# HGRN2 queries as two pairs of seven half-size products, between the transforms of the long convolutions

## The reference, cut to what matters

```python
proj = h @ p["w_in"]
(hg_q, hg_f_fwd, hg_f_bwd, hg_v, hg_g, ...) = _split(proj[..., D_CONV:], PLAIN_SPLITS)
uf = jnp.fft.rfft(uf32, n=2 * L, axis=1)
y = jnp.fft.irfft(uf * hf[None], n=2 * L, axis=1)[:, :L]
z = x1 * _fft_bidir_conv(v, filt[:, 0, 0], filt[:, 1, 0], p["hy_bias"][0])
y_a = x2 * _fft_bidir_conv(z, filt[:, 0, 1], filt[:, 1, 1], p["hy_bias"][1])
o_hg, s_hg = _scan_both_directions(
    _hgrn2_chunked, (heads(jax.nn.silu(hg_q), HG_DK), heads(hg_v, HG_DV)), ...)
```

## Time and profile before

| | us |
|---|---|
| median of 3 runs | 1392.11 (1391.52 to 1392.51) |
| profiled execution, first to last instruction | 1392.6 |
| TensorE busy in it | 1355.8 (97%) |
| VectorE busy | 600.6 |
| ScalarE busy | 390.8 |
| GpSimd busy | 313.7 |

### The profile page before, as it was taken

How to read it: one execution, slowest core, us unless ns; L and a number is a source line. 1 busy time by engine, 2 the same in 40 slices (tenths; PEclk the granted TensorE clock), 3 DMA queues, 4 the chain that set the end, 5 groups by cost and what they waited for, 6 DMA issues and landing times.

```text
span 1392.6 us, 20702 instructions
## 1 busy us (share of the span) xinstructions
PE 1355.8 (97%) x7716; PEld 950.3 (68%) x7716; DVE 600.6 (43%) x1347; ACT 390.8 (28%) x769; POOL 313.7 (23%) x248
## 2 busy tenths in 40 slices
PE   7999999999999999999999999999999999999996
PEld 2695898989988996788988875444445444444453
DVE  3467451885545486533322266333222332322224
ACT  3232221322544255233431141222112211221122
POOL 0431232243135553553333001101000000000001
PEclk9999999999999999999999999999999999999998
DMA  9640423133213336812144536999999999999992
GB/s 355 212 136 1 137 91 121 35 118 92 92 61 92 106 122 270 285 51 48 61 136 137 165 121 264 392 414 421 419 420 421 421 421 420 421 419 420 420 417 85
DMA packets 109744, 321.54 MB, mean 231 GB/s; under 512 B 12489, under 2 KB 72649, under 8 KB 81136
## 3 DMA queue, kind: packets, MB, share of 16 engines
q1 hardware_dynamic: 98416, 307.64, 57.6%
q0 software_dynamic: 2560, 8.81, 1.6%
q10 hardware_dynamic: 8704, 4.20, 1.1%
HBM read 320.08 MB, written 4.33 MB: 233 GB/s over the span
## 4 chain that ended last, share of the span: by engine, by line
PE 86%; DMA 9%; DVE 2%; ACT 1%; POOL 1%; issue 1%; SPq 0%; DVEq 0%; POOLq 0%
PE banks L650 21%; PE banks L617 20%; PE banks L2933 12%; DMA w<-in_exp_w 7%; PE banks L2980 7%; PE banks L2835 6%; PE banks L1057 3%; PE banks L2820 2%; PE banks L624 2%; PE banks L1201 1%; DMA ring<-in_ada_w 1%; PE banks L2828 1%; PE banks L769 1%; PE banks L889 1%; PE banks L701 1%; PE banks L1260 1%
## 5 line engine op out<-in xcount | busy, mean ns | idle before, releaser
L2933 PE MATMUL banks<-w,xg 128*64 128x512 f32 (+1 forms) x1312 | 235.8, 594 | 2.0 <-DMA w<-in_exp_w 1.9
L2933 PEld LDWEIGHTS banks<-w,xg 128*64 128x64 f32 (+1 forms) x1312 | 72.1, 126 | 150.9 <-issue 126.4
L650 PE MATMUL banks<-hT,ring 128*128 128x192 f32 x792 | 137.7, 327 | 0.2 <-DMA ring<-in_w_in 0.2
L3310 POOL DMA_INDIRECT fetched<-token_rows,row_of_place x32 | 32.1, 1004 | 443.2 <-DVE row_of_place L3111 433.1
L650 PEld LDWEIGHTS banks<-hT,ring 128*128 128x128 f32 x792 | 129.6, 190 | 2.1 <-DMA ring<-in_w_in 0.8
L2980 PE MATMUL banks<-w,hidT 128*64 128x512 f32 (+1 forms) x656 | 122.6, 600 | 0.3 <-DMA w<-in_exp_w 0.2
L2835 PE MATMUL banks<-y,selT 128*128 128x512 f32 x384 | 115.0, 415 | 0.0
L650 PE MATMUL banks<-x,ring 128*128 128x192 f32 x528 | 97.0, 327 | 0.9 <-ACT late L1377 0.9
L650 PE MATMUL banks<-x,combos 128*128 128x192 f32 x528 | 96.6, 326 | 0.0
L3122 DVE SCALAR_TENSOR_TENSOR hid<-banks,gslot,sil 128x256 f32<-128x256 f32 x33 | 16.0, 484 | 178.3 <-ACT sil L3015 177.7
L2835 PEld LDWEIGHTS banks<-y,selT 128*128 128x128 f32 x384 | 66.3, 189 | 35.1 <-issue 26.2
(11 more groups left out here) (482 smaller groups left out, 2033.4 us busy)
## 6 DMA issues: line engine op xcount, KB each, us to landing
w<-in_exp_w SPq DMA_DIRECT2D x198, 1024.0 KB, 13.9
ring<-in_w_in SPq DMA_DIRECT2D x46, 1024.0 KB, 5.5
ring<-in_ada_w SPq DMA_DIRECT2D x24, 1024.0 KB, 6.9
ring<-in_w_branch SPq DMA_DIRECT2D x8, 1024.0 KB, 6.6
ring<-in_w_out SPq DMA_DIRECT2D x4, 1024.0 KB, 6.6
arena<-in_sh_w SPq DMA_DIRECT2D x3, 1024.0 KB, 8.4
x<-in_x_sample SPq DMA_DIRECT2D x4, 512.0 KB, 8.3
token_rows<-whole_rows SPq DMA_DIRECT2D x3, 384.0 KB, 20.1
```

The costliest lines, as they stand in the source:

```text
L650: last = mm(out, lhsT=w[:, k, :], rhs=tokens[:, k, :], start=start and k == 0, stop=k == KD // 2 - 1, skip_group_check=not start)
L2933: ins = mm(ps[lo:hi, :], lhsT=xg[:, k, a_ * P + lo:a_ * P + hi], rhs=w13[:, a_, u, :, k, :], start=k == 0, stop=k == KD - 1)
L3310: nc.gpsimd.indirect_dma_start(fetched[:, a_, :], None, rows[:, :], bass.IndirectOffsetOnAxis(ap=row_of_place[:, 2 * a_:2 * a_ + 1], axis= ...
```

## The change

The queries join `PAIRS` between `hy_x2` and the forget gates. In each order TensorE runs `pair("hg_q", order)` in place of the two blocks of `project_T`. ScalarE keeps the partial results in `hq` itself; VectorE adds them up after that order's spectra, behind its wait for `s_spec`; and one silu over the whole of `hq` (128x1536), in place, follows the second `add_up`. VectorE waits for it (`s_queries`) before it adds up the first forget gates. The list of GpSimd's loop is `PAIRS`, so it prepares the queries' weights too.

```diff
@@ -419,7 +419,7 @@
-        PAIRS = [(name, h) for name in PAIRED[0:2] + FORGET for h in range(2)] + \
+        PAIRS = [(name, h) for name in PAIRED[0:2] + ("hg_q",) + FORGET for h in range(2)] + \
@@ -429,6 +429,8 @@
+            if name[0] == "hg_q":
+                return hq[:, 2 * name[1]:2 * name[1] + 2, :]
@@ -455,6 +457,7 @@
+        s_queries = sig("hgrn_queries_ready")
@@ -856,7 +859,7 @@
                 merge(0, order)
-                project_T("hg_q", "act", 2 * order, 2 * order + 2)
+                pair("hg_q", order)
                 pe.wait_ge(s_fconst.sem, 16 * N_FCONST)
                 pe.wait_ge(s_spec.sem, (order + 1) * NT)
@@ -1350,6 +1353,8 @@
             def block_sums_free(name):
 
+                if name[0] == "hg_q":
+                    return
@@ -1466,8 +1471,10 @@
                 merge_gate(0, j)
-                for c in (2 * j, 2 * j + 1):
-                    copy(hq[:, c, :], ("hg_q", c), ACT.Silu, src=banks.at(act, ("hg_q", c))[:, 0:T])
+                keep("hg_q", j)
+                keep_last("hg_q", j)
+            banks.emptied(act, ("hg_q", 1, "y"))
+            s_queries.on(on(flat(hq), flat(hq), ACT.Silu))
@@ -1981,6 +1988,7 @@
                 dve.wait_ge(s_spec.sem, s_spec.n)
+                add_up("hg_q", order)
                 if order == 0:
@@ -1993,7 +2001,7 @@
-            banks.emptied(dve, ("hg_q", CW - 1))
+            dve.wait_ge(s_queries.sem, 1)
             for name in FORGET:
```

## The result

| | before | changed |
|---|---|---|
| first comparison, median | 1392.31 us (6 runs, 1391.52 to 1395.13) | 1400.72 us (6 runs, 1396.89 to 1401.4) |
| ratio, 95% interval | | 1.0052 [1.0041, 1.0063] |
| second comparison, median | 1392.84 us (21 runs) | 1399.13 us (5 runs, 1398.32 to 1401.39) |
| ratio, 95% interval | | 1.0044 [1.0030, 1.0057] |
| profiled execution, span | 1392.6 us | 1399.6 us (first), 1399.0 us (second) |

The change made the kernel slower, as forecast, and by more: by the medians +8.4 us in the first comparison and +6.3 in the second, where the forecast was +5.25 and the range ended at +7.5. The ratios are taken over all runs and not from the two medians; that of the first comparison, 1.0052, is +7.2 us. So the median of 1400.72 lies 1.1 us above the range, and the time by the ratio just inside its upper end.

A forecast was written before the change was run, and what follows sets the result against it. TensorE was taken to bound the kernel, VectorE close behind. 2.44 us given back against new waits of 3.1 and 3.0 gave +3.65; one clock fall, 1.6, made +5.25 on 1392.11: 1397.4 us, range 1393.5 to 1399.6.

The forecast's parts named there:

- What bounds the kernel: Over the two convolutions, TensorE sets the time, with no wait ahead of either transform back; VectorE is close behind.
- the slack of VectorE: Ahead of the transforms back, VectorE's chain ends 1.50 us (order 0) and 2.56 us (order 1) before TensorE asks.
- The pair's own gain: Queries' products as a pair take 9.10 us, not 10.32: TensorE gains 1.22 us an order, 2.44 us in all.
- Four operations of GpSimd an order: Preparing weights for pairs puts four GpSimd operations among VectorE's eight long ones, costing 4.28 us an order.
- The price of a meeting: Each GpSimd operation beside a long VectorE one, both reading SBUF, costs VectorE 1.07 us; bounds nothing and 1.27.
- the old meeting at 108.08: In order 0, the forget gates' combinations no longer delay VectorE's L1962, which takes 0.95 us off its chain.
- What was costed at nothing: VectorE's adding up (about 1.2 us each time), ScalarE's copies and the silu (at most 1.7 us) delay nothing.
- Rival 1: VectorE's chain in both orders runs undisturbed by GpSimd; the whole 2.44 us stays, 1389.7 us; chance 9%.
- rival 2: Only two of four GpSimd operations an order meet VectorE's, 1391.5 us; with three, 1393.6; chance 13%, half for three.
- The clock: After one of TensorE's two new waits, its clock falls to half speed in the dense transforms, costing 1.6 us.
- the old fall: Clock drop at 391.80 in the profile before: 18 records took 3.83 us, not 2.34, so 1.5 us lost.
- two falls: The clock drops after both new waits ahead of the transforms back, costing 3.2 us: 1399.0 us; chance 18%.

The follow-up runs named there:

- foreign additions: Kernel before the change, with four unrelated GpSimd additions of 128x512 in SBUF added per order beside VectorE's long operations: 1398.76 us, ratio 1.0052.
- the two versions where nothing waits behind it: Changed kernel with GpSimd's three later operations held until the order's spectra, 1390.79 us; changed kernel with queries' pairs moved behind both convolutions, 1391.99 us.
- filler: Changed kernel with seven unused TensorE products ahead of each wait for the spectra: 1396.56 us, ratio 1.0026.
- held-back one: Changed kernel with GpSimd waiting for each order's spectra before preparing the next pair's weights: 1390.79 us, ratio 0.9986; again 1391.10 us, ratio 0.9993.

## Why the prediction was right, and where it was short

- **What bounds the kernel, and the slack of VectorE** (1.50 and 2.56 us): right. The four foreign additions met just this slack.
- **The pair's own gain**, 2.44 us: right; -2.43 and -2.44 in the two versions where nothing waits behind it.
- **Four operations of GpSimd an order, all among VectorE's long ones**: right, in place and number.
- **The price of a meeting**, 1.07 us: right for the first of an order, 2.29 - 1.22, but 0.95 for the three that follow (2.17 - 1.22). An order costs VectorE 3.9 us and not 4.28. The other row that I had, 0.95 for L1962, was as near, and a mean of the two would have been better. The waits, counted from start to start as in the forecast, were 2.80 and 2.69 us in place of 3.1 and 3.0 (2.63 and 2.52 as the profile counts idle time); the two shifts, without the late start, 1.57 and 1.54, together 3.11 in place of 3.65. By the rule of the Trainium skill ("SBUF — State Buffer", section "Who interferes with whom") taken literally, 1.27 each, the sum would have been further off.
- **That the old meeting at 108.08 goes**: right. No GpSimd operation stands there any more (idle for 16.46 us ahead of L2488), and the sum with it comes out.
- **What was costed at nothing**: right. The wait ahead of the second spectra is 0.78 us, where it was 0.79: `add_up` is covered. The silu has 1.48 us and ends 2.6 us after the second transform has begun, as its row in the timeline of ScalarE shows:

```profile
156.15 1.48 ACT L1477 ACTIVATE yT<-yT 128x1536 f32<-128x1536 f32 x1 [4.58 <-DVE yT L1839]
```

- **Rivals 1 and 2**: out. Rival 1 (VectorE undisturbed) is contradicted by four stretched rows an order; rival 2 does not occur by itself but has the size that I gave it. What I read for rival 1 was half right only: VectorE's eight long operations start some 1.14 us apart in four cases and 1.26 in the other three.
- **The clock** is the term that was mis-sized. I counted one fall at 1.6 us. The price was near, 1.7 (5.39 to 7.08, and 5.52 to 7.22; 1.5 with the foreign additions, 5.31 before to 6.78). Its source was a little short too: the 18 records that I put at 2.34 us at full clock have 2.16 in the profiles without that fall, so the old fall costs 1.7 and not 1.5. The number was too low. Idle times shorter than I had forecast, 2.6 and 2.5 us, were enough, and in the four profiles without filler that have waits of this length, two of the changed kernel and one each of two experiments, five of the six waits from 2.52 to 2.73 us were followed by a fall; those of 1.43, 0.74 and 0.63 us were not. The filler products put the average roughly at 2.6 us, one and a half falls, so two may well be as ordinary as one. With 3.1 for the meetings and two falls of 1.7 the sum is +6.5, against the second comparison's +6.3. I had given two falls 18% and one 33%, with the words that the number was a guess; the rows of one execution could not say more, and the range should have carried two falls further.
- **The remaining part of +8.4** in the first comparison, about 2 us over that sum by the medians and 0.7 by the ratio, isn't explained. The interval of its ratio, 5.7 to 8.8 us, and that of the second, 4.2 to 7.9, hold 6.5 both, so no further mechanism is needed, and none is excluded.

The forecast thus had the sign and the mechanism. One error, the meetings too dear by 0.5, took back part of the other, the clock too cheap by 1 to 1.8; that the sum came as near as it did is in this part luck.

## What to carry to other kernels

Before an operation is added on GpSimd, look what VectorE does at that time: if both read two operands in SBUF, each meeting costs VectorE most of GpSimd's operation (0.95 to 1.07 us of 1.27 here), and what waits for VectorE pays it, even when GpSimd itself is idle for most of the span. Where the addition isn't needed until later, one wait that holds it behind VectorE's chain can turn a loss into the intended gain. And to an idle time of TensorE of some 2.5 us ahead of dense work add the price of a fall of the clock, 1.5 to 1.7 us here after five waits of six; work that is of no use but keeps TensorE going was then cheaper than waiting.

## What the hardware showed that I had not expected

- VectorE and GpSimd alternate strictly in these rows, where both read two operands in SBUF: GpSimd's operations of 1.27 us have 2.13 to 2.25 us, VectorE's of 1.22 have 2.17 to 2.29, as long as both have work. A meeting costs VectorE 1.07 or 0.95 us: in the changed kernel the first of four has the higher price, with the foreign additions the first three in order 0 and the first two in order 1. What decides it stays open.
- The shortest operation of GpSimd still waits for VectorE's: two columns have 1.18 us beside a long operation and 0.20 between two, at no cost for VectorE.
- Memsets of GpSimd, 6.3 us of them, cost VectorE nothing.
- The clock fell to 0.50 after five of six idle times of TensorE of 2.5 to 2.7 us, and not after 0.63, 0.74 or 1.43 us. The Trainium skill ("TensorE: Matmul & The Clock Gate", section "HAM oscillation — how this bites in real kernels") tells of idle waits that drop the clock for the next burst; here it lasted 3.4 us of that burst.
- The fall that the earlier trace rows show comes in some executions only: in the first profile of the changed kernel and not in the second, in the first of the held-back ones and not in the second. From the levels' start to the product at 850.16 it is 614.9 us before and 615.0 in the held-back one, both with the fall, and 612.9 to 613.7 in five without (the second profile of the changed kernel, also without, has 615.0, of which 1.4 is one wait for a weight slab). So 1.5 us or so of the scatter between executions of one kernel has this cause.
